# Attention of a three-layer model in pairs of heads, with pieces of weight slabs and of the output matrix between the steps

## The reference, cut to what matters

```
sc = einsum(q, k) * scale + bias          # per head, causal
p  = softmax(sc);  o = einsum(p, v)       # 16 heads of 64 (layer 0: 8 heads x 3 branches, 4 pairs)
x  = x + concat(o) @ w_out
```

## Time and profile before

| | |
|---|---|
| time, median of 3 runs | 1293.44 us (1290.76 to 1293.54) |
| profiled execution | 1286.64 us, span 1284.8 us |
| PE busy | 1229.2 us, 96 % of the span |
| DVE busy | 812.0 us, 63 % |
| ACT busy | 591.8 us, 46 % |
| POOL busy | 146.4 us, 11 % |
| moved by DMA | 195.75 MB, mean 152 GB/s |

### The profile page before, as it was taken

How to read it: one execution, slowest core, us unless ns; L and a number is a source line. 1 busy time by engine, 2 the same in 40 slices (tenths; PEclk the granted TensorE clock), 3 DMA queues, 4 the chain that set the end, 5 groups by cost and what they waited for, 6 DMA issues and landing times.

```text
span 1284.8 us, 21781 instructions
## 1 busy us (share of the span) xinstructions
PE 1229.2 (96%) x9383; PEld 1159.3 (90%) x9383; DVE 812.0 (63%) x1243; ACT 591.8 (46%) x859; POOL 146.4 (11%) x83
## 2 busy tenths in 40 slices
PE   6979999999999999999999999999999988999997
PEld 5879558999999987899999998999996878999997
DVE  5256755877444655577743597786546667888842
ACT  4055744444333454444433446654426545665531
POOL 3000004000012000400002301310050011111000
PEclk8879859999999999999999999999998998999999
DMA  7963004555555543455555553454871353556550
GB/s 227 177 186 113 20 1 132 164 173 189 186 175 166 163 132 98 132 165 186 176 196 170 161 159 98 133 187 132 261 240 66 97 165 101 195 172 206 184 178 33
DMA packets 198563, 195.75 MB, mean 152 GB/s; under 512 B 9707, under 2 KB 196532, under 8 KB 198452
## 3 DMA queue, kind: packets, MB, share of 16 engines
q1 hardware_dynamic: 194276, 191.19, 47.8%
q10 hardware_dynamic: 4192, 3.17, 0.8%
HBM read 193.26 MB, written 1.48 MB: 152 GB/s over the span
## 4 chain that ended last, share of the span: by engine, by line
PE 83%; DVE 5%; DMA 4%; SPq 3%; POOL 2%; ACT 2%; issue 1%; ACTq 0%; DVEq 0%; POOLq 0%
PE ps_gemm L1522 70%; PE ps_score L1582 4%; PE ps_out L1616 4%; PE ps_trans L1598 2%; DMA f_bias<-cum_scr 2%; DMA raw<-in_ev_w_in 1%; PE ps_score L1776 1%; POOL f_bias L657 1%; SPq L553 1%; DMA raw<-in_w_in 1%; DVE act_lo L1016 1%; SPq L467 1%; PE ps_gemm L1675 1%; ACT w_hi L698 1%; DVE h_rnn L1337 1%
## 5 line engine op out<-in xcount | busy, mean ns | idle before, releaser
L1522 PE MATMUL ps_gemm<-act_hi,w_hi 128*128 128x256 f32 x1640 | 474.0, 289 | 33.0 <-DVE act_lo L1016 21.1
L1522 PE MATMUL ps_gemm<-act_lo,w_hi 128*128 128x256 f32 x1640 | 469.2, 286 | 0.0
L1522 PE MATMUL ps_gemm<-act_hi,w_lo 128*128 128x256 f32 x1640 | 468.8, 286 | 0.0
L1010 DVE TENSOR_TENSOR w_lo<-raw,w_hi 128x2048 fp32r<-128x2048 f32 (+1 forms) x179 | 406.9, 2281 | 72.0 <-ACT w_hi L698 71.7
L698 ACT ACTIVATE w_hi<-raw 128x2048 fp32r<-128x2048 f32 (+1 forms) x179 | 332.4, 1860 | 233.3 <-DMA raw<-in_mlp_w 113.1
L1522 PEld LDWEIGHTS ps_gemm<-act_hi,w_hi 128*128 128x128 f32 x1640 | 319.0, 195 | 40.4 <-issue 35.6
L1522 PEld LDWEIGHTS ps_gemm<-act_lo,w_hi 128*128 128x128 f32 x1640 | 319.1, 195 | 0.3
L1522 PEld LDWEIGHTS ps_gemm<-act_hi,w_lo 128*128 128x128 f32 x1640 | 318.9, 194 | 0.2
L1522 PE MATMUL ps_gemm<-hid_hi,w_lo 128*128 128x256 f32 x512 | 145.2, 284 | 0.0
L1522 PE MATMUL ps_gemm<-hid_hi,w_hi 128*128 128x256 f32 x512 | 145.1, 283 | 0.0
L1522 PE MATMUL ps_gemm<-hid_lo,w_hi 128*128 128x256 f32 x512 | 145.1, 283 | 0.0
(11 more groups left out here) (278 smaller groups left out, 1848.1 us busy)
## 6 DMA issues: line engine op xcount, KB each, us to landing
raw<-in_mlp_w SPq DMA_DIRECT2D x64, 1024.0 KB, 5.3
raw<-in_w_in SPq DMA_DIRECT2D x30, 1024.0 KB, 5.5
raw<-in_w_up SPq DMA_DIRECT2D x24, 1024.0 KB, 5.2
raw<-in_od_w_in SPq DMA_DIRECT2D x12, 1024.0 KB, 5.0
raw<-in_w_down SPq DMA_DIRECT2D x12, 1024.0 KB, 5.2
raw<-in_ev_w_in SPq DMA_DIRECT2D x9, 1024.0 KB, 10.9
...
```

The lines of the kernel that those rows point to most:

```text
L1010: dve.tensor_tensor(w_lo[:, slot, 0:k, 0:n], raw[:, slot, 0:k, 0:n], w_hi[:, slot, 0:k, 0:n].bitcast(F32), ALU.subtract).then_inc(w_ready, 1)
L1522: ins = pe.matmul(dst, lhs, rhs, start=(first and k == 0 and half == 0 and q == 0), stop=(last and k == n_k - 1 and q == 2), skip_group_ch ...
```

## The change

The units become pairs of heads (`att_pairs` in place of `att_units`). In a pair's step the scores of both heads are issued in turn (block 0 of the even head, block 0 of the odd head, block 1 of each), into one PSUM bank for each; the values likewise. DVE normalises both heads with one reciprocal and one product per block, with a factor broadcast along the row, and ACT copies both transposed heads in one instruction. The lags are one step (normalise), two (T), three (V and the parts of the output); the probability ring has 4 buffers in place of 5, and scores have one buffer per head.

The table `FILL` replaces `IN_STEPS`: it names, for each step, the parts of slabs (a slab with a range of its eight chunks) and chunks of the first two slabs of the output matrix that PE multiplies at the end of that step. What of the output matrix is done there is left out of `out_stage`. `gemm` takes a list of chunks, and flags whether the slab is opened and closed.

In layer 0 the slabs come in another order (keys and values to be compressed, first half of the queries, keys, gates, values of NSA, then the difference heads), six before the attention; `compress` comes before the attention too. The bias row is made at the start: its table is read on ACT's queue, and ACT's queue writes the row to DRAM, spread over the 16 copies in one transfer. SP issues x, three slabs, the parameters, two slabs, the eight bias transfers, the compress weights, lambda, and then the other slabs. The difference heads' norm is done once for all four: sums of squares as a column per head and block, one square root of 128x8, one reciprocal, eight small products that spread the factor, two DVE products.

```diff
-PB = 5
-LAG_N, LAG_T, LAG_V, LAG_HI, LAG_LO = 2, 3, 5, 6, 7
...
+PB = 4
-DQ0, DK0, DV0, DQ1, GATE, KV_CMP, DK1, DV1, SKW, Q0, Q1, SV = range(12)
+A_SLABS = [((512,), 256), ((0,), 256), ((768, 1024), 128), ((1280,), 24), ((896, 1152), 128), ((1304,), 256),
+           ((1816,), 256), ((1560,), 256), ((2072,), 256), ((2328,), 256), ((2584,), 256), ((256,), 256)]
+KV_CMP, Q0, SKW, GATE, SV, DQ0, DK0, DQ1, DK1, DV0, DV1, Q1 = range(12)
 TWO_LOADS = (SKW, SV)
-CMP1_STEP, CMP2_STEP = 3, 5
-A_GROUPS = [j + (j > DV1) + (j > Q0) for j in range(12)]
-CMP1_GROUP, CMP2_GROUP = DV1 + 1, Q0 + 2
-IN_STEPS = (
-    {1: 5, 2: 6, 3: 7, 4: 8, 5: 9, 6: 10, 8: 11},
-    {1: 3, 2: 4, 3: 5, 5: 6, 6: 7, 7: 8, 9: 9, 10: 10, 11: 11},
-    {2: 6, 5: 7},
+A_GROUPS = [0, 1, 2, 3, 4, 6, 8, 9, 10, 11, 12, 13]
+CMP1_GROUP, CMP2_GROUP, DN_GROUP = 5, 7, 14
+
+FILL = (
+    {0: [("in", DK0, 0, 8)], 1: [("in", DQ1, 0, 8)], 2: [("in", DK1, 0, 4)], 3: [("in", DK1, 4, 8), ("in", DV0, 0, 4)],
+     4: [("in", DV0, 4, 8)], 5: [("in", DV1, 0, 4)], 6: [("in", DV1, 4, 8)], 7: [("in", Q1, 0, 4)],
+     8: [("in", Q1, 4, 8)],
+     13: [("out", 0, (0, 1)), ("out", 1, (0, 1))], 14: [("out", 0, (4, 5)), ("out", 1, (4,))],
+     15: [("out", 1, (5, 6))], 16: [("out", 0, (6, 7)), ("out", 1, (7,))], 17: [("out", 0, (2,)), ("out", 1, (2,))]},
+    {0: [("in", 2, 0, 8), ("in", 3, 0, 8)], 1: [("in", 4, 0, 8)], 2: [("in", 5, 0, 8), ("in", 6, 0, 4)],
+     3: [("in", 6, 4, 8), ("in", 7, 0, 8)], 4: [("in", 8, 0, 8)], 5: [("in", 9, 0, 8), ("in", 10, 0, 8)],
+     6: [("in", 11, 0, 8)],
+     7: [("out", 0, (0, 1, 2)), ("out", 1, (0, 1, 2))], 8: [("out", 0, (3,)), ("out", 1, (3,))],
+     9: [("out", 0, (4,)), ("out", 1, (4,))], 10: [("out", 0, (5,)), ("out", 1, (5,))]},
+    {0: [("in", 6, 0, 8)], 2: [("in", 7, 0, 8)],
+     6: [("out", 0, (0,)), ("out", 1, (0,))], 7: [("out", 0, (1,)), ("out", 1, (1,))],
+     8: [("out", 0, (2, 3)), ("out", 1, (2, 3))], 9: [("out", 0, (4,)), ("out", 1, (4,))],
+     10: [("out", 0, (5,)), ("out", 1, (5,))]},
 )
-IN_BEFORE = (5, 3, 6)
+OUT_EARLY = [{j: [k for s in sorted(f) for part in f[s] if part[0] == "out" and part[1] == j for k in part[2]]
+              for j in (0, 1)} for f in FILL]
+IN_BEFORE = (6, 2, 6)
+DN_STEP = 10
...
+            for i in range(8):
+                units, pv = [], []
+                for h, r in zip((2 * i, 2 * i + 1), halves):
+                    bias = [nb[:, h, P:T], nb[:, h, :]] if p == 1 else [nb2[:, h, 0:P], nb2[:, h, P:384]]
+                    units.append(unit(qk[r, i, :], qk[r, 8 + i, :], bias))
+                    pv.append(full_pv([vv[:, tb, h * HD:(h + 1) * HD] for tb in range(TB)]))
+                g = st["m_in"].g0 + 3 * (i // 2) if p == 1 else st["r_qk"].g0 + 2 * (i // 2)
+                pairs.append(dict(kind="full", gate=None, out=i, start=True, stop=True, last=True, units=units, pv=pv,
+                                  qk_groups=(g, g + 1), v_groups=(g + 2,) if p == 1 else ()))
...
-        for j in range(RING):
+        for j in range(3):
             a_slab(j)
-        sp.dma_start(buck[:, :], t["bucket"]).then_inc(ld["bias"], 16)
-        sp.dma_start(btab[:, :], t["bias_table"]).then_inc(ld["bias"], 16)
...
-        for i, name in enumerate(("ev_lam_q1", "ev_lam_k1", "ev_lam_q2", "ev_lam_k2")):
-            sp.dma_start(lamv[:, i, :], t[name].to_broadcast([P, HD])).then_inc(ld["lam"], 16)
-        for i, name in enumerate(("k", "v")):
-            sp.dma_start(cw1[:, i, :, :], t[f"ev_cmp_w1_{name}"][0].rearrange("(m p) j -> p m j", p=P)).then_inc(ld["cw"], 16)
-        sp.wait_ge(brow_ok, 1)
-        sp.dma_start(scr_b, brow[:, :]).then_inc(brow_out, 16)
-        a_slab(RING)
+        a_slab(GATE)
+        a_slab(SV)
         sp.wait_ge(brow_out, 16)
-        sp.dma_start(scr_w, bass.AP(tensor=scr_b.tensor, offset=0, ap=[[0, 16], [1, 16 * REL]])).then_inc(brow_out, 16)
-        sp.wait_ge(brow_out, 32)
         for a in range(P // 16):
             src = bass.AP(tensor=scr_w.tensor, offset=P - 1 - 16 * a, ap=[[16 * REL - 1, 16], [REL, 16], [1, T]])
             sp.dma_start(nb[16 * a:16 * a + 16, :, :], src).then_inc(nb_in, 16)
         for i, name in enumerate(("k", "v")):
+            sp.dma_start(cw1[:, i, :, :], t[f"ev_cmp_w1_{name}"][0].rearrange("(m p) j -> p m j", p=P)).then_inc(ld["cw"], 16)
+        sp.wait_ge(xt, 4)
+        for i, name in enumerate(("k", "v")):
             for half in range(2):
                 sp.dma_start(cw2[:, i, half * HD:(half + 1) * HD], t[f"ev_cmp_w2_{name}"][0]).then_inc(ld["cw"], 16)
+        for i, name in enumerate(("ev_lam_q1", "ev_lam_k1", "ev_lam_q2", "ev_lam_k2")):
+            sp.dma_start(lamv[:, i, :], t[name].to_broadcast([P, HD])).then_inc(ld["lam"], 16)
         sp.dma_start(b_f, t["b_forget_2"].rearrange("a h -> h a"),).then_inc(ld["bf"], 16)
-        for j in range(RING + 1, 12):
+        for j in range(DQ0, 12):
             a_slab(j)
...
+        def attention(p, in_slab):
+            a, pairs, probs_t = att[p], PAIRS[p], prob_ts[p // 2]
+            n = len(pairs)
+            for i in range(n + 3):
+                if 2 <= i < n + 2:
+                    kind = pairs[i - 2]["kind"]
+                    act.wait_ge(a["tr"], i - 1)
+                    if i >= 3:
+                        act.wait_ge(a["pv"], i - 2)
...
                     else:
+                        ins = act.activation(probs_t[:, :, :], ps_t[:, :, 0:384], ACT.Copy)
+                    ins.then_inc(a["trc"], 1)
+                if i >= 3 and pairs[i - 3]["last"]:
+                    pr = pairs[i - 3]
+                    o, seq = pr["out"], pr["seq"]
+                    act.wait_ge(a["pv"], i - 2)
...
+                if i < n:
+                    for m, u in enumerate(pairs[i]["units"]):
+                        k = 2 * i + m
+                        act.wait_ge(a["logit"], k + 1)
...
+                        ins.then_inc(a["prob"], 1)
...
+        act.dma_start(buck[:, :], t["bucket"]).then_inc(ld["bias"], 16)
+        act.dma_start(btab[:, :], t["bias_table"]).then_inc(ld["bias"], 16)
+        act.wait_ge(brow_ok, 1)
+        act.dma_start(bass.AP(tensor=scr_w.tensor, offset=0, ap=[[REL, 16], [16 * REL, 16], [1, REL]]),
+                      brow[:, :].unsqueeze(1).to_broadcast([16, 16, REL])).then_inc(brow_out, 16)
...
+        compress()
+        a_slab(DQ0)
...
+            def normalise(i):
+                pr = pairs[i]
+                k = slice(2 * i, 2 * i + 2)
+                q = 2 * i % PB
+                dve.wait_ge(a["prob"], 2 * i + 2)
...
+                link(dve.reciprocal(fac[:, k, :], psum_[:, k, :]))
...
+                else:
+                    for b, (c0, w) in enumerate(pr["units"][0]["blocks"]):
+                        v = prob[:, q:q + 2, c0:c0 + w]
+                        ins = dve.tensor_tensor(v, v, fac[:, k, b:b + 1].to_broadcast([P, 2, w]), ALU.mult)
+                ins.then_inc(a["norm"], 1)
 
+            for i in range(n + 3):
...
+                if i < n:
+                    logits(i)
...
+                for part in FILL[p].get(i, ()):
+                    if part[0] == "in":
+                        in_slab(part[1], part[2] == 0, False)
+                if 1 <= i < n + 1:
+                    normalise(i - 1)
+                if i >= 3 and pairs[i - 3]["last"] and pairs[i - 3]["kind"] != "diff":
+                    pr = pairs[i - 3]
+                    o, seq = pr["out"], pr["seq"]
+                    dve.wait_ge(a["oh"], seq + 1)
+                    dve.tensor_tensor(lo[:, o, :], ps_o[:, seq % 2, 0:T], hi[:, o, :].bitcast(F32), ALU.subtract)\
+                        .then_inc(a["ol"], 1)
...
+                for part in FILL[p].get(i, ()):
+                    if part[0] == "in":
+                        in_slab(part[1], False, part[3] == KS)
...
+            if opens:
+                split_lo(s + AHEAD - 1)
+            if j == 1:
                 rms_tok(2)
-            if j % 3 < 2:
...
+        def attention(p, in_part, out_name, out_hi, out_lo, chunk_ready):
+            a, pairs, probs_t = att[p], PAIRS[p], prob_ts[p // 2]
+            n = len(pairs)
             def scores(i):
+                pr = pairs[i]
+                for g in pr["qk_groups"]:
+                    pe.wait_ge(emptied[g % 2], out_count(g))
+                if i:
+                    pe.wait_ge(a["logit"], 2 * i)
+                for b in range(TB):
+                    for m, u in enumerate(pr["units"]):
+                        c0, w = u["blocks"][b]
+                        ins = pe.matmul(ps_s[:, m, c0:c0 + w], u["q"][:, b * P:(b + 1) * P], u["k"][b], start=True, stop=True)
                 ins.then_inc(a["score"], 1)
             def transposes(i):
+                pr = pairs[i]
+                pe.wait_ge(a["norm"], i + 1)
+                if i:
+                    pe.wait_ge(a["trc"], i)
+                for m in ((1,) if pr["kind"] == "diff" else (0, 1)):
+                    k = (2 * i + m) % PB
```

(73 more changed lines are left out.)

488 lines of the change are left out of this document (198 added, 290 removed).

## The result

The changed kernel takes 1252.17 us (median of 5 runs, 1244.96 to 1255.85), 0.9694 of the kernel before (95 % interval 0.9651 to 0.9736): some 40 us less, where 16 had been forecast and 1260 was the lower end of the range. The profiled execution took 1244.96 us, span 1243.2, against 1286.64 and 1284.8.

The account below looks back on a forecast made before the run. PE (TensorE) was taken as the bound nearly everywhere. First attention -6.7, second -12.3 and third +3 summed to -16.0 us, taken from the median 1293.44 to forecast 1277 us, range 1260 to 1296.

Parts of the forecast that it names:

- the price of a slab: Gemm on PE: a slab of 48 matmuls takes 5.95 us, 0.124 each, 0.74 per 128-row chunk.
- the section on costless edits: Four probability buffers for five, rms_tok at slab 1 and ScalarE's new order were costed at nothing.
- First stage: Before the first attention: compress starts at about 64 at 1.2 GHz, attention at about 87.6 us, bounds 74 and 92.
- Rival 2: First stage ends at 74, bias being issued 13 us sooner: 13.6 us more gain, 1264 us; chance 0.10.
- Pairs: Attention on PE: two heads' S, V and T take 2.5 us against 4.24, array halves running side by side.
- Rival 4: Array halves do not overlap when heads alternate matmul by matmul: +26 us, 1319 us; chance 0.07.
- Bare step: A pair's attention step without slab or matrix work takes 5.1 us, set by DVE.
- First attention: With its matrix: end 204.2 against 219.86 at full clock, half clock costs +9, so -6.7 us; bounds -15.7 and +9.3.
- rival 1: The clock stays at 2.4 GHz in bare steps: -27 us, 1266 us; chance 0.20.
- Rival 3: Clock falls to 1.2 GHz until attention ends, in the first and third stage: +12 us, 1305 us; chance 0.13.
- Second attention: With its output matrix, every step filled: 104.5 us instead of 116.8, -12.3 us; bounds -13 and +2.
- Third attention: From the first logits: +1 us at full clock, 2 added for bare steps at 1.2 GHz, +3; bounds -2 and +15.

Follow-up runs that it names:

- b_shift: The kernel before with one unused tile of 64 bytes per partition placed ahead of x: 1271.99 us, ratio 0.9869 to the kernel before.
- c_after: The changed kernel, unedited, run again as a control: 1250.84 us, ratio 0.9703 to the kernel before.
- a_noshift: The changed kernel with its two small norm tiles at the end of the memory instead of ahead of x: 1269.99 us, ratio 0.9864 to the kernel before.
- c_before: The kernel before, unedited, run again as a control with its own profile: ratio 1.0021.
- a_p192: a_noshift with an unused tile of 192 bytes placed ahead of x: 1248.75 us, ratio 0.9667 to the kernel before.
- a_p32: a_noshift with an unused tile of 32 bytes placed ahead of x: ratio 0.9681 to the kernel before.
- s_serial: a_noshift with a pair's score and value matmuls issued head by head instead of alternating: 1270.24 us, ratio 0.9867 to the kernel before.
- s_noout: a_noshift with no output matrix chunks between the attention steps, all coming after the attention: 1295.86 us, ratio 1.0065 to the kernel before.

## Why the prediction was wrong

The sum of the parts was nearly right, and one sentence under it was wrong. The step that failed is the price of a slab, "48 matmuls, 5.95 (0.124 each, so 0.74 per 128-row chunk of 6)", which was taken over unchanged for the changed kernel, together with every stage outside the diff at no difference. Two small tiles in the list of memory places, which the section on costless edits did not even name, made 120.0 ns into 117.8 or 113.3: 17 to 19 us (b_shift's ratio; c_after's 1250.84 against a_noshift's 1269.99). None of the signs that the prediction named for being wrong came: a pair's S took 0.86 us and not 1.7, the second stage gained more than 8 us, the first attention started inside 74 to 92. What failed was a price that none of them watched.

With that term taken out, a_noshift against c_before, profiled executions, by the forecast's own terms:

| term | forecast | measured |
|---|---|---|
| first attention starts | 87.6 | 87.63 |
| its matrix ends | 213.2 (204.2 at full clock): -6.7 | 208.80: -12.8 against c_before (-11.1 against the first profile) |
| second attention with matrix | -12.3 | -10.3 (121.94 for 132.20) |
| third attention | +3 | +5.2 (78.64 for 73.43) |
| all else | 0 | -0.3 |
| sum | -16.0 | -18.2 (1268.3 for 1286.5) |

That the sum came so near is in part luck: the first attention gave 6.1 us more than forecast, the two others together 4.2 less. Each is read from one execution, and in the profiles of the changed kernel and its variants that keep the chunks the first attention with its matrix takes 118.4 (a_p192) to 124.4 us (a_p32).

- **First stage: right** in its order and times: table load forecast at 62.4, seen at 62.10; `compress` at 1.2 GHz forecast at 64 for 14 us, seen at 63.90 for 13.88. Rival 2 did not come.
- **Pairs: right.** S 0.86 and V 0.80 as taken; T 0.66 where 0.81 was taken, for which no row stood; the pair's 2.32 lies below its bound of 2.5. Rival 4 falls, and s_serial shows that the halves do not need to alternate.
- **Bare step: right.** The chain of one in the kernel after, from S to the next S, is 4.96 us (5.1 forecast), with DVE holding 2.58 of it (144.64 to 147.22): normalise 0.10 + 0.17 + 1.04.

```profile
143.76 0.88 PE ps_score L1626 x8
...
144.66 0.29 DVE prob L1066
...
145.86 0.10 DVE fac L1078
...
145.99 0.17 DVE fac L1081
...
146.18 1.04 DVE prob L1095 x2
...
147.26 0.87 PE ps_trans L1638 x6
148.14 0.58 PE ps_out L1653 x8
148.72 0.76 PE ps_score L1626 x8
```

The Trainium skill's rule on this ("TensorEngine Tiling (Array Packing)", Performance Considerations, PSUM Bottleneck), that tiling does not speed up what empties PSUM, is borne out by that chain, where the logits, which read the scores out of PSUM, take 1.20 us (144.66 to 145.86) beside 0.88 of S. A step without other matrix work is so set by DVE, and s_noout's third attention shows what that costs: 88.96 us against 73.43 with single heads.

- **First attention: direction right, size off.** Half clock was put at +9; the matrix ended 4.6 after the 204.2 of full clock. The clock was at 1.2 GHz for about 17 us (150.7 to 160.9 and 167.8 to 174.6), which is between rival 1 and the forecast. It came back the second time 2.9 us after the first chunks (171.7). Rival 3 did not come in the kernel as it is; in s_noout, without the chunks, something near it did: 1.2 GHz from 164.3 to 198.4, and in the third stage from 980.1 to 1017.6.
- **Second attention:** from the first S to the matrix's end it is 104.2 us, forecast 104.5. What was missed lies ahead: with two slabs before it instead of three the first S waits for DVE to empty the second one, behind two `split_lo`. The chain of a_noshift:

```profile
408.40 2.29 DVE w_lo L1026
410.69 0.60 DVE m_qk L1285
411.29 2.20 DVE w_lo L1026
413.49 0.07 DVE rs_tok L1046
413.56 0.61 DVE m_qk L1285
...
414.31 1.65 PE ps_score L1626 x8
```

From the first slab's activations to that S there are 17.75 us, to the same point (third slab's start) 15.4 in c_before; 2.4 of the forecast gain go there. That 104.2 then met 104.5 is in part luck: 6.8 us of it ran at 1.2 GHz (413.5 to 420.4, and so the S of 1.65), which the forecast had not, and pairs at 2.32 us for 2.5 made up for some of it.
- **Third attention: direction right, size off.** The forecast added 2 us for bare steps at 1.2 GHz. The clock is there from 963.1 to 980.1: two bare steps of 7.06 us (963.87 to 970.93 is the first) and part of a third, which at 4.96 us would be some 5 us less. Moving two chunk pairs into these steps takes 4.4 us of the stage back.
